# A stick-breaking head's rounded copy made by VectorE in place of ScalarE, in a two-layer hybrid attention trunk

## The reference

```python
for i in range(S // BLOCK):
    end = (i + 1) * BLOCK
    qb = qh[:, :, i * BLOCK:end]
    z = jnp.einsum('bhqd,bhkd->bhqk', qb, kh[:, :, :end]).astype(jnp.float32) * scale
    strict = s_pos < t_pos
    log_beta = jax.nn.log_sigmoid(z)
    log_1m = jnp.where(strict, -jax.nn.softplus(z), 0.0)
    suffix = lax.cumsum(log_1m, axis=3, reverse=True) - log_1m
    a = jnp.where(strict, jnp.exp(log_beta + suffix), 0.0)
    outs.append(jnp.einsum('bhqk,bhkd->bhqd', a, vh[:, :, :end]))
```

## Time and profile before

| | |
|---|---|
| median of 3 runs | 1207.55 us (1207.02 to 1207.75) |
| profiled execution: its own time | 1207.45 us |
| its span, first to last instruction | 1205.6 us |
| PE busy | 1159.9 us, 96% of the span |
| DVE, ACT, POOL busy | 565.1, 570.0, 575.5 us (47%, 47%, 48%) |
| attention stages | about 60 to 210 us and 650 to 815 us of the span |

### The profile page before, as it was taken

One profiled execution on the slowest core, in us unless ns is written; L12 is line 12 of the kernel. 1 busy time (PEld: TensorE's weight loads), 2 busy tenths in 40 slices (PEclk: granted clock), 3 DMA queues, 4 the chain that ended last, 5 costly groups with the idle time before them and its releaser, 6 DMA issues.

```text
span 1205.6 us, 15300 instructions
## 1 busy us (share of the span) xinstructions
PE 1159.9 (96%) x5566; PEld 971.7 (81%) x5566; DVE 565.1 (47%) x759; ACT 570.0 (47%) x833; POOL 575.5 (48%) x292
## 2 busy tenths in 40 slices
PE   6999998999999999999999999799999999999996
PEld 4788887878888888888888889687788888888885
DVE  6756667775222222222455676758642222222225
ACT  5777888444223223133446888855331322322421
POOL 4355562664434444444644455546544343444450
PEclk9999999999999999999999999999999999999998
DMA  5220100322322323222322121102332233232322
GB/s 184 71 71 25 64 28 25 105 78 97 105 94 99 105 87 104 97 94 87 100 75 70 36 88 35 36 30 76 121 107 88 93 99 105 87 104 87 105 70 70
DMA packets 30009, 99.63 MB, mean 83 GB/s; under 512 B 3712, under 2 KB 5760, under 8 KB 29952
## 3 DMA queue, kind: packets, MB, share of 16 engines
q1 hardware_dynamic: 28656, 96.75, 24.0%
q10 hardware_dynamic: 1296, 2.13, 0.5%
HBM read 96.77 MB, written 2.10 MB: 82 GB/s over the span
## 4 chain that ended last, share of the span: by engine, by line
PE 78%; DVE 7%; ACT 6%; issue 3%; POOL 2%; DVEq 1%; DMA 1%; POOLq 1%; ACTq 1%
PE DW L412 22%; PE DW L414 22%; PE DW L413 22%; PE Z L553 2%; PE Z L412 2%; PE Z L414 2%; PE Z L413 2%; DVE stage L1109 1%; DVE xm L991 1%; PE DW L497 1%; PE Z L541 1%; POOL w L883 1%; DMA x<-in_x 1%; ACT probs L796 1%; PE O L566 1%
## 5 line engine op out<-in xcount | busy, mean ns | idle before, releaser
L883 POOL TENSOR_TENSOR w<-raw,w 128x1024 fp32r<-128x1024 f32 x178 | 433.0, 2435 | 388.9 <-ACT w L659 379.3
L659 ACT ACTIVATE w<-raw 128x1024 fp32r<-128x1024 f32 x177 | 185.8, 1052 | 218.8 <-PE DW L414 198.7
L412 PE MATMUL DW<-xm,w 128*128 128x512 f32 x512 | 200.7, 392 | 5.1 <-POOL w L883 2.7
L412 PE MATMUL DW<-stage,w 128*128 128x512 f32 x512 | 199.4, 389 | 0.0
L413 PE MATMUL DW<-xm,w 128*128 128x512 f32 x512 | 199.2, 389 | 0.0
L414 PE MATMUL DW<-xm,w 128*128 128x512 f32 x512 | 199.2, 389 | 0.0
L414 PE MATMUL DW<-stage,w 128*128 128x512 f32 x512 | 199.2, 389 | 0.0
L413 PE MATMUL DW<-stage,w 128*128 128x512 f32 x512 | 199.2, 389 | 0.0
L1193 DVE TENSOR_TENSOR kf<-o 128x512 f32<-128x512 f32 x64 | 60.7, 949 | 192.9 <-ACT o L834 192.7
L1209 DVE TENSOR_TENSOR DW<-DW,probs 128x512 f32<-128x512 f32 x62 | 43.4, 700 | 224.1 <-PE DW L414 224.1
L412 PE MATMUL DW<-xa,w 128*128 128x512 f32 x296 | 118.9, 402 | 11.3 <-DVE xa L991 11.3
(11 more groups left out here) (214 smaller groups left out, 1666.6 us busy)
## 6 DMA issues: line engine op xcount, KB each, us to landing
raw<-in_weights SPq DMA_DIRECT2D x180, 512.0 KB, 3.3
x<-in_x ACTq DMA_DIRECT2D x8, 256.0 KB, 8.4
out_x<-x SPq DMA_DIRECT2D x16, 128.0 KB, 1.9
other<-in_positions SPq DMA_DIRECT2D x1, 256.0 KB, 3.7
gains<-in_gains ACTq DMA_DIRECT2D x1, 28.0 KB, 4.6
inv_freq<-in_inv_freq SPq DMA_DIRECT2D x1, 0.5 KB, 4.3
sinks<-in_sinks SPq DMA_DIRECT2D x1, 8.0 KB, 7.0
```

The source lines that it names most:

```text
L412: pe.matmul(bank, w[:, slot, 0, k], rhs[:, 0, c], start=start, stop=False)
L659: act.activation(w[:, slot_of(at_layer), 0], raw[:, p % 2], ACT.Identity).then_inc(w_hi, 1)
L883: pool.tensor_tensor(w[:, slot, 1], raw[:, p % 2], w[:, slot, 0].bitcast(F32), ALU.subtract).then_inc(w_ready, 1)
```

## The change

The step XH moves from ScalarE's code to VectorE's. The lists stay as they are, so XH keeps its place among the steps, but it is now VectorE that comes to it, waits for XE (`z_drained`) and for BA of the head before, and writes the copy. ScalarE no longer drains after XE.

```diff
@@ ScalarE
                         act.wait_ge(zx_full, l * SB_HEADS + n + 1)
                         act.activation(work[:, n % 2], Z[n], ACT.Exp).then_inc(z_drained, 1)
-                    elif step == "XH":
-                        act.drain()
-                        if n:
-                            act.wait_ge(o_full, l * O_USES + plan.o_use["BA", n - 1] + 1)
-                        act.activation(at[:, 0], work[:, n % 2], ACT.Identity).then_inc(sb_ahi, 1)
                     elif step == "BO":
@@ VectorE
                         dve.tensor_tensor(sp[:, 1], work[:, n % 2], sp[:, 0].bitcast(F32), ALU.subtract
                                           ).then_inc(sb_split, 1)
+                    elif step == "XH":
+                        dve.wait_ge(z_drained, l * SB_HEADS + n + 2)
+                        if n:
+                            dve.wait_ge(o_full, l * O_USES + plan.o_use["BA", n - 1] + 1)
+                        dve.tensor_copy(at[:, 0], work[:, n % 2]).then_inc(sb_ahi, 1)
                     elif step == "BD":
```

## The result

The changed kernel takes 1216.01 us (median of 4 runs, 1215.13 to 1217.49) against 1207.47 us: ratio 1.0073, 95% interval 1.0057 to 1.0089. It is 8.5 us slower; 1213.7 with a range of 1209.5 to 1217.5 was forecast. The profiled execution took 1215.13 us (span 1213.4), 7.7 us more than that of before. The weights are split and moved as before, so the place to look is again the attention stages.

A forecast was written before the change was run, and what follows sets the result against it. PE's idle time in the attention stages, 16.6 us, was taken to bound any gain, not a loss. Terms (a) to (g) summed to +6.25 us on 1207.45, giving 1213.7 us, 0.5% slower; range 1209.5 to 1217.5.

The forecast's parts named there:

- The bound: PE's idle time in the two attention stages, 9.0 and 7.6 us: 16.6 us limit a gain, nothing limits a loss.
- (a): Layer 0, head 0: XH0 between WR0 and WN0 holds the port, WN0 ends later and WT0 waits: +0.35 us.
- (b): Layer 0, head 1: BH2 comes earlier, BL2 asks for the port before XL1, PE's wait before BX2 goes: -1.4 us.
- (e): Layer 1, head 4: XH4 ahead of WM7 and BD3 delays both, and WA6 waits for BD3's drain: +0.5 us.
- (f): Layer 1, head 5: XH5 goes between ML0 and BL6, for which BX6 waits: +0.6 us.
- (g): Layer 1, head 6: XH6 comes after OE1, XL6 ends later at 803.0, and BA6 waits: +0.8 us.
- (c): Layer 0, head 5: early XL5 takes the port between MN2 and MN3, delaying BX6: +3.2 us, plus 0.7 of low clock.
- Rival 1: Layer 0, head 5: XL5 doesn't get between MN2 and MN3; sum +2.6 us, 1210.0 us; chance 0.12.
- rival 4: The copy runs at one element per cycle, or the low clock lasts longer than in (c): 1216.5 us and more; chance 0.12.
- (d): Layer 1, head 3: XH3 waits for CL17 on the port, TE14 and WL5 come behind it, WS6 starts later: +1.5 us.
- The other nine: 0: Copies at the nine remaining heads cost nothing: PE has a projection tile ahead, or (c) covers head 6 of layer 0.
- Faster: Rival 3: ScalarE, rid of 20.4 us, brings BH earlier, so waits before BX go: 1204.2 us; chance 0.06.

The follow-up runs named there:

- the kernel with nine copies: Changed kernel with the copies of layer 0 heads 0, 5 and layer 1 heads 1, 3, 4, 5, 6 back on ScalarE: 1207.49 us, ratio 0.9999.

## Why the prediction was right, and where it was short

- **The bound** was read rightly: only PE's idle time in the attention stages moved, by 1.5 us in the first and about 4.6 in the second, out of 7.7. Another 1.2 is the lower clock in BX6 and BA5 of layer 0, during which PE counts as busy; the last 0.4 is not traced.
- **The price of the copy** (0.83 us, from rows 4 and not from BP) and **that it asks for the port** (by its likeness to BL): both hold, the first by the median of 0.827, the second by CL17. The Trainium skill's rule (SBUF — State Buffer, Who interferes with whom) that a copy in a two-port mode takes the shared pair exclusively agrees with the 1.81 us here. The 0.73 us that the prediction worked out from the Trainium skill's cycles (VectorE: DVE Perf Modes, The TRN2 errata) does not: 0.827 was measured.
- **(a), (b), (e), (f), (g)** came within 0.3 us each, and (a) as it was put: WN0, 1.04 us before, lasted 1.53.
- **(c)**, the largest, came out as 3.2 + 0.9 where 3.2 + 0.7 was said. It rested on one pair of rows, read so that the engine that asks first goes first, even between two operations back to back; holding XL5 back shows it. The part of the clock was luck in its closeness: behind the same 6.3 us of waiting five executions lost between 0 and 1.3 us in BX6 and BA5 (last section), and all of BX6 at the low level, as the prediction had it, came in two of them. Rival 1 falls with XL5 between MN2 and MN3, and rival 4 in its first half with the copy's 0.827 us. One bound was summed wrong: at full clock (c) would be 2.4 us less by the earlier trace rows, not 2.1.
- **(d) was mis-sized**: 2.3, not 1.5. The step that failed is "XL2 ... may push CL17 back by as much again", left out of the sum. XL2 lasted 4.12 us behind BL3 in place of 3.12 and ended 0.8 us later. It reaches CL17 through VectorE: a small operation of WM5 is held until XL2 ends (1.02 us long before, 1.01 now), and behind it WE5, WR5, WN5 and CL17 moved by 0.8, and the copy had to wait that much longer. The rows of before, then of the changed kernel, POOL and DVE each:

```profile
722.97 3.12 POOL L929 TENSOR_TENSOR stage<-work,stage 128x1280 fp32r<-128x1280 f32 x1 [4.42 <-ACT stage L780]
...
725.10 1.02 DVE L1139 SCALAR_TENSOR_TENSOR small<-small,neg_sink 128x4 f32<-128x4 f32 x1
```

```profile
726.03 4.12 POOL L924 TENSOR_TENSOR stage<-work,stage 128x1280 fp32r<-128x1280 f32 x1 [4.21 <-DVE stage L1110]
...
729.16 1.01 DVE L1139 SCALAR_TENSOR_TENSOR small<-small,neg_sink 128x4 f32<-128x4 f32 x1
```

- **"The other nine: 0" failed at one of nine.** The step that failed is "PE has a projection tile in front of the step that wants it": for head 1 of layer 1 I had the delay of VectorE's queue, but not that it puts WM3's small operations under RM9 and the operation behind it on GpSimd, which hold them. PE then loses 0.34 us before BA1 and 0.49 before BS3, +0.8.
- These two make 1.6 of the 2.3 us between the forecast and the median. The rest was not traced in the executions at the median; the profiled one, the shortest of the four, is 0.9 us under it, and clock losses of that size come and go between executions (last section).
- **Faster** had its mechanism right in one place and no more: of 20.4 us that ScalarE lost, PE got 1.7.

## What to carry to other kernels

Moving work between engines with fixed queues changes two things at every place: who stands behind it on the new engine, and what its earlier or later end sets free on a third one. Price each place by the wait that ends last there, and look for back-to-back operations with two inputs in SBUF: an operation of GpSimd that is released into their midst can cost nearly its whole length (here XL5, 3.27 us long, cost 2.7). A move that loses as a whole may win at one or two places, and a neighbour's order at the port can undo it by 0.05 us, so try the winning places together with their neighbours.

## What the runs showed of the hardware that had not been expected

A wait of PE can cost more than its length, through the clock, and not in every execution. In the repeated run of the changed kernel WS6 of layer 1 lasted 3.3 us in place of 2.0, after 2.2 us in which PE stood idle; the profile of that run, by stretch, shows the idle time and then the 1.2 GHz level:

```profile
738.50:740.70 2.20, 0.20 (x1) 0.20 (x2) 1.87 (x3) 2.13 (x2) 2.08 (x1) 1.00 0.73 236
740.70:744.30 3.60, 3.60 (x18) 3.55 (x18) 0.18 (x1) 1.51 (x2) 0.83 (x1) 0.53 0.03 6
```

In the first profiled execution the same wait was followed by full clock (WS6 1.95 us):

```profile
741.10:744.50 3.40, 3.35 (x22) 3.13 (x23) 1.16 (x1) 1.78 (x2) 1.09 (x1) 1.00 0.03 7
```

That makes a difference of 1.3 us between two executions of one kernel, of the size of their scatter (1215.1 to 1217.5 us).

Nor does the length of the wait alone decide. BX6 of layer 0 in the kernel with nine copies, behind a wait of 3.10 us, and in the repeated run of the changed kernel, behind 6.31 us:

```profile
194.29:199.47 5.18, 5.18 (x20) 4.99 (x21) 4.06 (x6) 5.06 (x7) 2.78 (x1) 0.50 0.01 2
```

```profile
197.95:202.36 4.41, 4.41 (x21) 4.22 (x21) 4.15 (x7) 2.96 (x3) 0.00 (x0) 0.60 0.01 2
```

BX6 and BA5 together lasted 5.67 us before. Behind 6.3 us of waiting five executions lost 0.0, 0.2, 0.5, 1.2 and 1.3 us against that; behind 3.1 us four of five, the kernel before among them, lost nothing and one lost 1.0; behind 3.6 us the one execution lost nothing. A longer wait made the loss more frequent here, and no single execution tells its size.

And an operation on four columns with both inputs in SBUF, 0.16 us by itself, is held by the port as a large one is (0.55 and 0.33 us above, and 1.02 us behind XL2).
